# Row norms' factor per token in partitions, spread by ones times a diagonal; second GLU and pool products in another order

## The reference

```python
def rmsnorm(x, g):
    y = xf * lax.rsqrt(jnp.mean(xf * xf, axis=-1, keepdims=True) + EPS)
    return y.astype(x.dtype) * g
...
    h = rmsnorm(x, norm_mix)
    qa, ka, va, ub, cq, ckv, kpe, ud, gate_in = split_cols(h @ w_in)
    ud = ud[..., :CONV_WIDTH] * jax.nn.sigmoid(ud[..., CONV_WIDTH:])     # GLU, then conv 31, LayerNorm, silu
    merged = sum over four branches of sigmoid(gate) * (branch @ w_o)    # window, pooling, latent attention, conv
    x = x + merged @ w_out
    x = x + (silu(rmsnorm(x, norm_ffn) @ wg) * (rmsnorm(x, norm_ffn) @ wu)) @ wd
```

## Time and profile before

| | us |
|---|---|
| median of 3 runs | 2376.43 (2376.19 to 2378.64) |
| the profiled execution | 2380.27 |
| its span in the trace | 2378.50 |
| TensorE, matmuls busy | 2271.5 (96%) |
| VectorE busy | 1316.6 (55%) |
| ScalarE busy | 863.2 (36%) |
| GpSimd busy | 970.1 (41%) |
| mean granted clock of TensorE | 0.981 of 2.4 GHz |

### The profile page before, as it was taken

How to read it: one execution, slowest core, us unless ns; L and a number is a source line. 1 busy time by engine, 2 the same in 40 slices (tenths; PEclk the granted TensorE clock), 3 DMA queues, 4 the chain that set the end, 5 groups by cost and what they waited for, 6 DMA issues and landing times.

```text
span 2378.5 us, 39615 instructions
## 1 busy us (share of the span) xinstructions
PE 2271.5 (96%) x14968; PEld 2183.2 (92%) x14968; DVE 1316.6 (55%) x2350; ACT 863.2 (36%) x1684; POOL 970.1 (41%) x988
## 2 busy tenths in 40 slices
PE   6999999999999999999989999999999989999996
PEld 6999898888999999999989989988889989999996
DVE  7995444333337835727599765433332387275364
ACT  3015233444314534525421153334441245254352
POOL 4554354232564342333445444533326623333231
PEclk8999999999999999999999999999999989999998
DMA  5252122011222222222233411211113312222221
GB/s 177 80 182 79 36 72 67 27 41 41 85 101 80 72 89 72 91 70 85 63 130 138 126 52 54 71 50 41 41 32 106 113 52 91 70 89 89 72 80 54
DMA packets 70565, 187.84 MB, mean 79 GB/s; under 512 B 19825, under 2 KB 22481, under 8 KB 69393
## 3 DMA queue, kind: packets, MB, share of 16 engines
q1 hardware_dynamic: 62608, 165.64, 21.5%
q10 hardware_dynamic: 7808, 20.16, 2.5%
HBM read 173.47 MB, written 14.14 MB: 79 GB/s over the span
## 4 chain that ended last, share of the span: by engine, by line
PE 84%; DVE 11%; ACT 2%; issue 2%; DMA 0%; ACTq 0%; SPq 0%; DVEq 0%
PE gemm L681 41%; PE gemm L1143 17%; PE gemm L1133 14%; PE side L1143 3%; DVE rstd L1715 2%; PE side L1016 2%; PE side L996 1%; DVE act_lo L2168 1%; PE side L1003 1%; DVE side L1832 1%; PE side L947 1%; DVE prod L1762 1%; PE side L780 1%; PE side L867 1%; DVE prod L1922 1%
## 5 line engine op out<-in xcount | busy, mean ns | idle before, releaser
L661 POOL TENSOR_TENSOR ring_lo<-w_raw,ring_hi 128x512 fp32r<-128x512 f32 x232 | 308.1, 1330 | 588.9 <-ACT ring_hi L1574 588.8
L642 POOL CAST w_hi<-w_raw 128x384 fp32r<-128x384 f32 x376 | 218.3, 581 | 754.0 <-PE gemm L681 719.5
L644 POOL TENSOR_TENSOR w_lo<-w_raw,w_hi 128x384 fp32r<-128x384 f32 x376 | 447.8, 1191 | 30.1
L681 PE MATMUL gemm<-h_hi,w_hi 128*128 128x320 f32 x1664 | 420.8, 334 | 15.8 <-DVE conv_sample L1795 6.0
L681 PE MATMUL gemm<-h_lo,w_hi 128*128 128x320 f32 x1664 | 382.4, 311 | 0.0
L681 PE MATMUL gemm<-h_hi,w_lo 128*128 128x320 f32 x1664 | 382.4, 311 | 0.0
L681 PEld LDWEIGHTS gemm<-h_hi,w_hi 128*128 128x128 f32 x1664 | 285.8, 191 | 48.2 <-issue 21.6
L1143 PE MATMUL gemm<-act_hi,ring_hi 128*128 128x320 f32 x960 | 300.0, 313 | 18.8 <-issue 9.9
L1143 PE MATMUL gemm<-act_lo,ring_hi 128*128 128x320 f32 x960 | 299.2, 312 | 0.0
L1143 PE MATMUL gemm<-act_hi,ring_lo 128*128 128x320 f32 x960 | 299.2, 312 | 0.0
L681 PEld LDWEIGHTS gemm<-h_lo,w_hi 128*128 128x128 f32 x1664 | 281.6, 190 | 0.0
(11 more groups left out here) (296 smaller groups left out, 4265.3 us busy)
## 6 DMA issues: line engine op xcount, KB each, us to landing
w_raw<-in_ws_ff SPq DMA_DIRECT2D x120, 512.0 KB, 3.3
w_raw<-in_ws_gate SPq DMA_DIRECT2D x64, 512.0 KB, 3.3
w_raw<-in_ws_in SPq DMA_DIRECT2D x44, 512.0 KB, 3.3
w_raw<-in_ws_proj SPq DMA_DIRECT2D x64, 256.0 KB, 2.6
w_raw<-in_ws_out SPq DMA_DIRECT2D x16, 512.0 KB, 3.2
w_raw<-in_ws_fd SPq DMA_DIRECT2D x16, 384.0 KB, 3.0
x_park<-x ACTq DMA_DIRECT2D x2, 2560.0 KB, 12.4
x<-x_park ACTq DMA_DIRECT2D x4, 1280.0 KB, 6.0
```

Of the source, the lines that this page charges most:

```text
L642: eng.tensor_copy(w_hi[s][:, cols], w_raw[s][:, cols]).then_inc(w_high.sem, 1)
L644: eng.tensor_tensor(w_lo[s][:, cols], w_raw[s][:, cols], w_hi[s][:, cols].bitcast(F32), ALU.subtract).then_inc(w_split.sem, 1)
L661: eng.tensor_tensor(lo, src, hi.bitcast(F32), ALU.subtract).then_inc(lo_plain.sem, 1)
L681: mm = eng.matmul(dst[:, hf, 0:HALF], w, r[k][:, cols] if r in (xu_hi, xu_lo) else r[:, k, cols], start=first and k == 0 and part == 0, st ...
```

## The change

*The factor.* `layer_norm_sum` now uses each 128 tokens of `ssum` as weights and one column of ones as the moving operand: five products give a 128x5 block, tokens in partitions. ScalarE takes its root into `rcol`, VectorE the reciprocal, then VectorE multiplies the identity by each column (tokens 0 to 383, then 384 to 639; in the buffer `prod1`), and `spread_factor` multiplies that by a matrix of ones, which puts each token's factor in all partitions; ScalarE copies it to `rstd`. On TensorE `spread_factor` stands before the fourth tile of unit 1 (layer 0), before the last tile of unit 0 (layer 1), before the fourth tile of feed-forward unit 1, and at the end. `sqrt_table` is a root of one column on ScalarE that brings the table load ahead of the sum. The three small norms are left as they were. `ident` is loaded with the first constants, before x. On VectorE `first_out(0)` goes behind the first normed tile.

*The GLU.* `glu(1)` comes behind 6 steps of the convolution, `glu(2)` behind 30 more and `glu(3)` behind 24 more; four of the five memsets go from before `glu(0)` to behind those 30 steps.

*The pool products.* Gate unit 5 stands before the third pool product; the fourth stands within gate unit 6, behind six of its tiles. ScalarE reads gate unit 5 before the third pool product.

*The moved splits.* At the start of the quads `up_out(1)` goes ahead of the low parts of A11 and S3 and ahead of block A12, and the sum S4 goes behind the second summed weight.

```diff
-    u = [(("norm", 0, h), 4 + h) for h in range(2)]
+    u = [(("nsum", 0), 4), (("norm", 0, 0), 5), (("norm", 0, 1), 4)]
...
+        rcol, at = sb("rstd_tokens", [P, T // P], F32, at)
...
+        spreads = [(0, 0, 3), (1, 3, T // P)]
...
-            for dst, src in ((gmix, "g_mix"), (relb, "rel_bias"), (hot, "hot"), (ones, "ones")):
+            for dst, src in ((gmix, "g_mix"), (relb, "rel_bias"), (hot, "hot"), (ones, "ones"), (ident, "ident")):
...
-                for hf, cols in halves:
-                    fill(l, ("norm", a, hf))
-                    eng.matmul(B[4 + hf][:, 0:HALF], ones[:, :], ssum[:, cols], start=True, stop=True)\
-                       .then_inc(side.sem, 1)
+                bank = fill(l, ("nsum", a))
+                for j in range(T // P):
+                    mm = eng.matmul(bank[:, j:j + 1], ssum[:, j * P:(j + 1) * P], ones[:, 0:1], start=True, stop=True)
+                mm.then_inc(side.sem, 1)
+
+            def spread_factor(l, a):
+
+                for g, first, last in spreads:
+                    eng.wait_ge(spread_ready.sem, spread_ready.at(l, 2 * a + g + 1))
+                    bank = fill(l, ("norm", a, g))
+                    eng.matmul(bank[:, 0:(last - first) * P], ones[:, :], t2b[:, first * P:last * P],
+                               start=True, stop=True).then_inc(side.sem, 1)
...
+                            if l and k == KT - 1:
+                                spread_factor(l, 0)
+                        elif l == 0 and k == 3:
+                            spread_factor(l, 0)
...
                 first_gate(4)
+                first_gate(5)
                 pool(2)
-                first_gate(5)
+                first_gate(6, 0, 6)
                 pool(3)
-                first_gate(6)
+                first_gate(6, 6, KT)
...
-                for u in range(1, 4):
+                ff_unit(1, hu_tile, lambda k: spread_factor(l, 1) if k == 3 else None)
+                for u in range(2, 4):
...
+            def sqrt_table():
+
+                eng.activation(unused[:, :], eps[:, :], ACT.Sqrt)
+
             def stds(l, name, width):
                 for hf, cols in halves:
                     bank = filled(eng, l, name(hf))
                     eng.activation(rstd[:, cols], bank[:, 0:HALF], ACT.Sqrt, bias=eps[:, :], scale=1.0 / width)\
                        .then_inc(freed(name(hf)), 1)
 
+            def row_factor(l, a):
+                bank = filled(eng, l, ("nsum", a))
+                eng.activation(rcol[:, :], bank[:, 0:T // P], ACT.Sqrt, bias=eps[:, :], scale=1.0 / DM)\
+                   .then_inc(freed(("nsum", a)), 1)
+                for g, first, last in spreads:
+                    bank = filled(eng, l, ("norm", a, g))
+                    eng.activation(rstd[:, first * P:last * P], bank[:, 0:(last - first) * P], ACT.Copy)\
+                       .then_inc(freed(("norm", a, g)), 1)
...
+            sqrt_table()
...
-                stds(l, lambda hf: ("norm", 0, hf), DM)
+                row_factor(l, 0)
...
+                sqrt_table()
                 cast(5)
                 eng.wait_ge(ln_scaled.sem, ln_scaled.at(l, 4))
-                stds(l, lambda hf: ("norm", 1, hf), DM)
+                row_factor(l, 1)
...
+            def row_factor(l, a):
+
+                evacuated(eng, l, ("nsum", a))
+                eng.reciprocal(rcol[:, :], rcol[:, :]).then_inc(rstd_ready.sem, 1)
+                eng.wait_ge(rstd_ready.sem, rstd_ready.at(l, 4 * a + 1))
+                for g, first, last in spreads:
+                    n = last - first
+                    eng.tensor_tensor(t2b[:, first * P:last * P].rearrange("p (j t) -> p j t", j=n),
+                                      ident[:, :].unsqueeze(1).to_broadcast([P, n, P]),
+                                      rcol[:, first:last].unsqueeze(2).to_broadcast([P, n, P]), ALU.mult)\
+                       .then_inc(spread_ready.sem, 1)
+                evacuated(eng, l, ("norm", a, 0))
+                evacuated(eng, l, ("norm", a, 1))
...
-                first_out(0, sg)
                 for k in range(KT):
                     if k >= 2:
 
@@ -1761,6 +1809,8 @@
                     gain = gmix[:, l * KT + k:l * KT + k + 1]
                     eng.scalar_tensor_tensor(t2[k % 2][:, :], x[:, k, :], gain, rstd[:, :], ALU.mult, ALU.mult)\
                        .then_inc(t_ready.sem, 1)
+                    if k == 0:
+                        first_out(0, sg)
...
-                eng.memset(pbp[:, :, 0:PH], 0.0).then_inc(hist_zeroed.sem, 1)
-                eng.memset(ntk[:, :, :], 0.0).then_inc(pads.sem, 1)
-                eng.memset(kT[64:128, 0, :], 0.0).then_inc(pads.sem, 1)
-                eng.memset(kT[0:64, 1, :], 0.0).then_inc(pads.sem, 1)
...
-                    last = min(done + 24, 2 * TAPS * (i + 1)) if i < 3 else 8 * TAPS
+                    last = done + (6, 30, 24)[i] if i < 3 else 8 * TAPS
                     conv(done, last)
                     done = last
+                    if i == 1:
+                        eng.memset(pbp[:, :, 0:PH], 0.0).then_inc(hist_zeroed.sem, 1)
+                        eng.memset(ntk[:, :, :], 0.0).then_inc(pads.sem, 1)
+                        eng.memset(kT[64:128, 0, :], 0.0).then_inc(pads.sem, 1)
+                        eng.memset(kT[0:64, 1, :], 0.0).then_inc(pads.sem, 1)
...
-                act_block(af[A12], 4, lo_half)
-                act_sum(af[S4][:, :, :], af[A12][:, :, :], af[S2][:, :, :], ALU.subtract, 19)
+                up_out(1)
                 act_low(A11)
                 act_low(S3)
-                up_out(1)
                 sum_low(FF_QUADS[0] + 1)
+                act_block(af[A12], 4, lo_half)
                 sum_low(FF_QUADS[0] + 2)
+                act_sum(af[S4][:, :, :], af[A12][:, :, :], af[S2][:, :, :], ALU.subtract, 19)
```

More of the change, by code:

```diff
@@ L103, in _bank_uses @@
     u += [(("Sv", NB - 1), 6 + (NB - 1) % 2), ("Su", 4)]
-    u += [(("norm", 1, h), 4 + h) for h in range(2)]
+    u += [(("nsum", 1), 4), (("norm", 1, 0), 5), (("norm", 1, 1), 4)]
     table, seen = {}, {4: 0, 5: 0, 6: 0, 7: 0}
@@ L1202, in _ @@
             layer_norm_sum(L, 0)
+            spread_factor(L, 0)
         def filled(eng, l, name):
```

25 lines of the change are left out of this document (14 added, 11 removed).

## The result

| | before | after |
|---|---|---|
| median, us | 2377.53 (4 runs) | 2353.60 (2352.15 to 2355.77, 4 runs) |
| ratio | | 0.990, 95% interval 0.9883 to 0.9917 |
| the profiled execution | 2380.27 | 2355.77 |
| its span | 2378.50 | 2354.0 |

A forecast was written before the change was run, and what follows sets the result against it. TensorE's work sets the time, with some 107 us of stops to win from. Terms -0.4 + 6.2 + 5.5 + 14.0 + 1.5 + 2.9 = 29.7 us gave 2346.7 us, by way of 2350.6 and the runs' median; range 2338 to 2358.

The forecast's parts named there:

- The pool products: Gate units: a whole unit ahead of the third pool product covers its 3.9 us wait, 3 to spare; 14.0 us gained.
- The second GLU: Convolution, unit 5: TensorE's waits of 2.84 and 3.2 us and slow stretches behind them go; 4.5 and 4.9 us gained.
- rival e: Third GLU comes late, so TensorE stops there instead and its clock falls: 6 us less gain, 2353; 5%.
- The feed-forward start: Block products' start: stop moves from first block to third, VectorE's work unchanged; 1.5 us gained, bounds -4 and +4.
- The new factor: Row norms at five places: one-column sums, small root and reciprocal, diagonal spread replace the old chain; about 6 us gained.
- Layer 0: Start of layer 0: factor ready near 34.3 instead of 35.9, TensorE resumes at 41.3 instead of 42.54; 1.7 us gained.
- The end: Last row norm: sum to first scaled output tile takes 4.5 us instead of 7.43; 2.9 us gained.
- (a): Feed-forward starts worsen: ScalarE's blocked queue, VectorE colliding with GpSimd; each costs 3 us instead of gaining: 2354; 13%.
- (b): New factor helps only at the end: one-column passes at upper bound, TensorE awaits the diagonal at the spread: 2351; 12%.
- (d): Slower than before: thin one-column passes drop TensorE to 1.2 GHz behind four inner places, three slow units each: 2431; 2%.
- (c): Clock stays up: TensorE keeps 2.4 GHz at layer starts and block products: 2339; 8%.
- (f): Exposed table loads cost more than their row; each moved off the path gives 1.4 us more: 2344; 2%.

The follow-up runs named there:

- the two other pairs: With against without the new factor: the changed kernel, 2353.60 against 2354.79 us; the same with early first copy and reordered low parts, 2349.81 against 2351.01 us.
- the run with the quads' new order: Changed kernel with ScalarE's first block-product copy early and VectorE's low parts of summed weights 4, 5 ahead of next quad's weight sums: 2349.81 us.

## Why the prediction was right, and where it was not

- **What bounds.** Held: four stops per layer, two of them removable. The edits of the pool and GLU, 23.4 of the 29.7 us forecast, measured 23.5 alone. The time is in the range because of these two; the other 6.3 us of the forecast measured about nothing. Two of the prediction's own signs of being wrong showed: a wait of TensorE on the diagonal (1.3 us, at the end) and a granted clock of 0.50 behind the one-column products (layer 0).
- **The pool products**, 14.0: measured 13.4 alone, 6.4 and 7.0 by stages. The cover held, no wait is left there; the "3 us to spare" were not measured.
- **The second GLU**, 4.5 and 4.9 us: 10.1 alone. The gain by stages, 4.35 and 4.4, exceeds the waits alone (2.84 and 3.2), so the slow stretch behind the stop was rightly part of it. The third GLU was not late (rival e): the time of 2353 that I gave it came true by another way.
- **The feed-forward start**, 1.5 us: it gave -0.7 and 0.0 by the table (44.31 and 44.97 to 45.02). The splits alone gave 0.3 and 1.0; the factor took 0.4 to 1.9 us per layer back. The stop moved to the third block as forecast. But the weight's low part of the fifth block, which ended the stop at 787.47, was not "within 0.7 us of its old time": it was done 40.3 us behind the sum for 41.5, and VectorE's sums behind it, stretched beside GpSimd, made the sixth block late instead. "VectorE has the same work as before" was the step that failed: the same instructions took longer. The factor did come earlier, and was lost in VectorE's next instructions, block A11, which took 3.79 us beside GpSimd's splits for 1.93 in the kernel before, where the split began 1.45 us behind it:

```profile
753.94 1.93 DVE L2158 SCALAR_TENSOR_TENSOR act<-x,vec,rstd 128x320 f32<-128x320 f32 x4
```

```profile
742.58 3.79 DVE L2209 SCALAR_TENSOR_TENSOR act<-x,vec,rstd 128x320 f32<-128x320 f32 x4
742.29 2.80 POOL L665 TENSOR_TENSOR ring_lo<-w_raw,ring_hi 128x512 fp32r<-128x512 f32 x2 [6.61 <-ACT ring_hi L1607]
```

  (The first row is of the kernel before, the others of the changed one.) In all eight profiles with the factor VectorE could scale 5.65 us behind the sum and A11 took 3.78 or 3.79 us; in all six without it these were 7.31 and 1.93: 1.7 us won, 1.9 lost.
- **The new factor** failed: -0.4 + 1.7 + 0.6 + 2.9 = 4.8 us forecast outside the feed-forward part, and with it measured at -0.8 to 1.2 as a whole. Term by term:
  - *One more DMA before x*, -0.4 us: the first product began at 4.5 to 4.9 us in the eight profiles with `ident` ahead, at 3.9 to 4.2 in the six without: 0.6, mis-sized a little.
  - *Layer 0*, +1.7: nothing alone (163.16 for 163.16), and between -1.0 and +1.4 with the GLU moved. The working had unit 1 at full speed behind the sum, the third tile done at 32.7 and the copies at 34.3; in this profile they came at 36.3. Unit 1's end was put at 38.1, which counts the spread's 0.9 us but not the low clock (until 33.79); it came at 40.3. VectorE's low tile behind it then took 2.16 us for 0.81 before, and TensorE resumed at 44.15, where 41.3 was forecast.
  - *Layer 1*, +0.6: 0.8 alone, 0.1 and 2.5 in the two other pairs, in a row that wanders by 2 us. Nothing speaks against it, and nothing shows it.
  - *The end*, +2.9: 1.3 in this profile, 1.9 where the sum ran at the full clock. I took 1.3 us for the ones products and copies at the low clock; the rows show 3.02, from 2337.06 to 2340.08:

```profile
2333.91 1.89 PE L704 MATMUL side<-ones,gate 128*128 128x1 f32 x10 [2.64 <-DVE gate L1789]
2337.06 2.50 PE L712 MATMUL side<-prod,ones 128*128 128x384 f32 x4 [1.26 <-DVE prod L1760]
...
2340.08 1.68 DVE L2329 SCALAR_TENSOR_TENSOR prod<-x,gain_final,rstd 128x640 f32<-128x640 f32 x2 [2.74 <-ACT rstd L1261]
```

  Four passes of 384 and 256 columns at half clock are 2.50 us. The old sum's four passes have as many columns, and their 1.34 us at the full clock, doubled, would have given it. The rest of the working, 3.2 us up to there, held (3.15).
- **The rivals.** (a), a worse feed-forward start, is nearest by number, 2354, but by luck: it asked for 3 us lost per layer, and 0.7 and 0.0 were; the collision with GpSimd that it named is in the rows above. (b), the factor brings nothing but at the end, was right in its outcome, at 12%, and its 2351 is nearest by what happened, though not by its reasons: ten passes took 1.3 us at the full clock and 2.1 at half, not the upper bound, and TensorE waited for the diagonal at the end alone. (d), the clock behind the thin products, showed its first sign (3.4 us slow, not the 21 us it needed, and the clock had fallen before them). (c) was wrong: the clock still fell. (f): in the old chain the root began 2.20 us behind the sum's start (2357.11 to 2359.31), in the run with the quads' new order, where the sum ran at the full clock, 1.39 us behind it. So the root came 0.8 us sooner, less than the 1.28 of the load's row, since it now waits for the whole sum (1.28 us), where the old load began 0.90 us behind the sum's start, at 2358.01. Nothing beyond the row was won. The Trainium skill (ScalarE: Activation LUTs, What ACT_TABLE_LOAD costs) would have added a drain of 1.38 us to each; the rows do not show it.
- The Trainium skill's rule on VectorE and GpSimd (SBUF — State Buffer, Who interferes with whom) spoke against layer 1, and the rows agree: with `first_out(1)` out of the way, VectorE's tile took 2.08 us beside GpSimd for 0.88 alone.

## What to carry to other kernels

Before you shorten a chain, look for the next wait behind its last instruction in the same queue: here `first_out(1)` waited for an end on TensorE that the new chain even made later. Look also at what the instructions will run beside once they come earlier: at the feed-forward start the factor's whole lead went to GpSimd's splits. Rebuilding the row norm brought nothing measurable. Moving a whole unit of TensorE's work ahead of a product that waits is cheap, adds up, and can be priced within 1 us from one profile, the slow clock behind the stop included. When an engine's order holds one product, moving the wanted instruction ahead gives what the rows say at that place (4 us per layer here), but expect part of it back if that engine is also full: the time fell by 3.8 us in all, not by 8.

## What was not expected of the hardware

- The clock at one place differs from one execution to the next of the same code: in layer 0 the ten one-column passes took 2.12 or 2.13 us in four profiles and 1.28 to 1.48 in three. Unit 1 behind them was slow for over 3 us in the four and for 3 us in one of the three. The Trainium skill (TensorE: Matmul & The Clock Gate, Part 1) says that the number of slow products at a start varies between runs of one kernel. These seven are different kernels, but their code is the same up to there, and they agree.
- Ten passes with one column took 1.28 us at the full clock, where the same sum in four passes of 320 columns took 1.24 to 1.34. With 64 columns the ten took 1.36. The thin moving operand saved nothing.
- TensorE kept busy with products that nobody reads (21 of 320 columns, in a stretch of 5.3 us) did not keep its clock: it read 0.50 from 2330.5 on, 2.4 us behind the sum's start, and without them from 2331.4, 2.5 us behind it.
- VectorE's four instructions of block A11 at the feed-forward start took 1.93 us or 3.79, by where GpSimd's splits lay beside them, and did so alike in all six profiles without the factor and all eight with it.
